# The sums of squares of queries and keys in the second block, as one full-precision matmul or as two rounded ones

## The chip, the cores and the metric

The kernel runs on one core of a Trainium2 chip. Its time is the device time of one execution in microseconds (us). Five engines work side by side, each in the order of its own program: TensorE (PE in the profile; its weight loads are PEld) multiplies, VectorE (DVE) and ScalarE (ACT) work on tiles, GpSimd (POOL) is a slower one of that kind, and SyncE (SP) issues the transfers from memory. They wait for each other by semaphores. Matmuls read the on-chip memory (SBUF) and write to the eight banks of PSUM; ACT and DVE take the results out of the banks.

## The reference

Two blocks stand behind each other: a mixer with a mixture of experts (32 experts, 256 tokens of 1024 numbers), and a second block with two kinds of attention and a feed-forward part. The change touches one step of the second block, the length to which the queries and keys of the gated delta rule are brought:

```python
def l2norm(x):
    xf = x.astype(jnp.float32)
    return xf * lax.rsqrt(jnp.sum(xf * xf, axis=-1, keepdims=True) + EPS_2)

proj = jnp.einsum('bsd,de->bse', hn, w_in[l])
(fq, fk, fv, ff, gq, gk, gv, ga, gb, gz, gate_fox, gate_gdn) = split_in(proj)
qkv = jax.nn.silu(causal_dwconv(jnp.concatenate([gq, gk, gv], axis=-1), gdn_conv_w[l]))
cq, ck, cv = jnp.split(qkv, [GDN_K_WIDTH, 2 * GDN_K_WIDTH], axis=-1)
q = l2norm(cq.reshape(B, S, GDN_HEADS, GDN_HEAD_K))
k = l2norm(ck.reshape(B, S, GDN_HEADS, GDN_HEAD_K))
```

There are 8 heads of 128 numbers and 256 tokens. The result goes on to the delta rule, then the outputs of both attentions to a projection and the feed-forward part.

## The kernel before, in words

The second block's attention part is the function `phase_c`. It goes through the 8 heads in two groups of 4 (`hg` is 0, then 1). In a group TensorE makes the projections in this order: gq, gk, gv (delta rule), fq, then the sums of squares ("ss"), then rows of gates spread over all partitions ("rb"), then fk, the products of keys and queries ("kq"), transposes, fv, gz, and behind them a chain of small matmuls that inverts a triangular matrix.

**Precise products from rounded parts.** Most large products are made in the rounded type (fp32r). A weight or an activation is taken apart into a high part (rounded) and a low part (what is left, rounded), and the product is three rounded matmuls. The weights come through SP's queue into a ring of two buffers and are taken apart unit by unit, each unit 128 x 1024: ACT makes the high part (L183, a cast), and the low part (L186, a subtraction) is made by VectorE for the even units and by GpSimd for the odd ones. High and low parts have four buffers each, so a cast waits until TensorE has used the unit four before it. `units.ahead(engine, who, n)` stands in each engine's program where that engine is to make the parts up to unit n + 3. A projection (`columns`) is four units. In the first group fq is units 12 to 15 and fk units 16 to 19, in the second group 40 to 43 and 44 to 47.

**The sums of squares.** The queries and keys, turned so that a head's 128 numbers lie in the partitions, are in `gT` (4 tiles of 128 x 512 for queries and keys of a group). ACT squares them (L1957) into `X` and `XT`, two tiles each, which `sq(j)` names. TensorE sums over the partitions with a matrix of ones (L2361). Both operands are plain fp32, and one such matmul is two MATMUL instructions in the trace. ACT turns the sums to 1/root by Ln (L1971) and Exp (L1975), and VectorE multiplies `gT` by it (L2206); TensorE needs that for kq, behind fk. TensorE's rb matmuls (L2367) come directly behind the sums and read only 8 rows of the array (8x512 operands).

**Order of the work around it.** All orders are written out by hand. ACT, behind the Silu of gv: 4 squares, cast of unit 17 (45), fq's first half out of its bank (L1964), casts of units 18 and 19 (46, 47), fq's second half, then Ln and Exp. VectorE: low part of units 16 and 18 (44 and 46), then the rows of rb (L2199), then L2206. GpSimd: low part of units 17 and 19 (45 and 47). `yf` and `yg` hold the outputs of the two attentions, each as a pair [0] (high) and [1] (low); the second half of their rows is first written at the end of the second group. `yf[0]` also serves early on for the parts of the small gate weights, which `wg2_high` and `wg2_low` name.

Of the kernel before, what the change touches and what calls it, by code (L numbers as in the profile page):

```python
# [27 lines left out]
F32 = mybir.dt.float32  # L28
F32R = mybir.dt.float32r
I32 = mybir.dt.int32  # L30
U32 = mybir.dt.uint32
ALU = mybir.AluOpType
# [3 lines left out]
P = 128  # L36
# [1606 lines left out]
HG = 4  # L1643
# [150 lines left out]
def phase_c(nc, A, sem, sb, ring, banks, k, env):  # L1794
    x, xn, hT, ident, tri, ones, sel, prm2, units, hTh, hTl, yf, yg, prm1, prow1, prow2, stat = (
        env[n] for n in "x xn hT ident tri ones sel prm2 units hTh hTl yf yg prm1 prow1 prow2 stat".split())
# [22 lines left out]
    def sq(j):  # L1819

        return (X, XT)[j // 2][:, j % 2].rearrange("p h n -> p (h n)")

    vb = sb("vb", [P, NT, HG, P])

    wg2 = X.rearrange("p t h n -> p (t h) n")
    wg2_high, wg2_low = (yf[0][:, 4 * i:4 * i + 4, :].rearrange("p c (a n) -> p (c a) n", a=2) for i in range(2))
# [41 lines left out]
    with nc.Block() as block:  # L1868
# [18 lines left out]
        def _(act):  # L1887
            chain = Chain(act, sem("actC"))
# [47 lines left out]
            for hg in range(2):  # L1936
# [19 lines left out]
                for j in range(4):  # L1956
                    act.activation(sq(j), gT[:, j // 2, 2 * (j % 2):2 * (j % 2) + 2, :].rearrange("p h s -> p (h s)"),  # L1957
                                   ACT.Square).then_inc(sem("g_sq"), 1)
                if hg == 0:
                    banks.moved(act, ("nm", KC // 2 - 1))  # L1960
                for j in range(2):
                    ahead(u0 + 12 + 2 * j + 2)
                    bank = banks.take(act, ("fq", hg, j))
# [5 lines left out]
                for j in range(4):  # L1969
                    bank = banks.take(act, ("ss", hg, j))  # L1970
# [7 lines left out]
                for h in range(HG):  # L1978
                    act.wait_ge(sem("dlog"), 4 * hg + h + 1)
                    act.activation(attnT[:, :, h, :], attnT[:, :, h, :], ACT.Exp).then_inc(sem("dexp"), 1)  # L1980
                    bank = banks.take(act, ("rb", hg, h))
                    act.activation(egb[:, h, :], bank[:, P:S], ACT.Exp).then_inc(sem("egb"), 1)
                for j in range(2):
                    ahead(u0 + 16 + 2 * j + 2)
                    bank = banks.take(act, ("fk", hg, j))
                    last = act.copy(fqk[:, 1, 2 * j:2 * j + 2, :], bank.rearrange("p (h s) -> p h s", h=2))
                    banks.release(last, ("fk", hg, j))
                for t in range(NT):
                    ahead(u0 + 20 + (3, 4)[t])
                    bank = banks.take(act, ("fv", hg, t))  # L1990
                    banks.release(act.copy(fv[:, t, :], bank), ("fv", hg, t))
                for t in range(NT):
                    bank = banks.take(act, ("x1", hg, t))
                    banks.release(act.copy(X[:, t], heads(bank)), ("x1", hg, t))
                for t in range(NT):
                    ahead(u0 + 24 + (3, 4)[t])
                    bank = banks.take(act, ("gz", hg, t))
                    banks.release(act.activation(gz[:, t, :], bank, ACT.Silu), ("gz", hg, t))
                for l in range(1, LEVELS):
                    for t in range(NT):  # L2000
                        bank = banks.take(act, ("t1", hg, l, t))
                        banks.release(act.copy(T1[:, t, :], bank), ("t1", hg, l, t))
                        if l > 1:
                            bank = banks.take(act, ("tr", hg, l, t))
                            banks.release(act.copy(XT[:, t], heads(bank)), ("tr", hg, l, t))

                for h in range(HG):
                    if h == HG - 1:
                        bank = banks.take(act, ("u0", hg))
                        banks.release(act.copy(u[:, 0], heads(bank)), ("u0", hg))  # L2010
                    act.wait_ge(sem("fmax"), 4 * hg + h + 1)
                    bank = banks.take(act, ("lo", hg, h))
# [5 lines left out]
                bank = banks.take(act, ("wT", hg))  # L2018
                banks.release(act.activation(wTn[:, :, :], heads(bank), ACT.Copy, scale=-1.0), ("wT", hg))
                bank = banks.take(act, ("st", hg))  # L2020
                banks.release(act.copy(state[:, :, :], heads(bank)), ("st", hg))
                bank = banks.take(act, ("u1", hg))
                banks.release(act.copy(u[:, 1], heads(bank)), ("u1", hg))
                for h in range(HG):
                    bank = banks.take(act, ("pt", hg, h))
                    banks.release(act.copy(probT[:, h, :], bank[:, 0:384]), ("pt", hg, h))
                for j in range(2):
                    bank = banks.take(act, ("pv", hg, j))
# [5 lines left out]
            for w, buf in (("gf", sgf), ("gg", sgg)):  # L2034
                for j in range(2):
                    ahead(UNITS_E + 4 * (w == "gg") + 2 * j + 2)
                    bank = banks.take(act, (w, 0, j))
# [8 lines left out]
        @block.gpsimd  # L2046
        def _(g):
            chain = Chain(g, sem("poolC"))
            g.wait_ge(sem("norm_scaled"), k.scaled("nm") + NT)
            units.ahead(g, "low1", -2)  # L2050
            g.memset(X[:, :, :, :], 0.0).then_inc(sem("wg2_zeroed"), 1)
            chain(g.memset(eps2[:, :], EPS2))
            chain(g.memset(lm[:, :, :], 0.0))
            for l in range(LEVELS):
                if l == 1:
                    g.wait_ge(sem("low0_split"), units.before["low0"] + 1)
                    units.ahead(g, "low1", 0)
                b = 1 << l
                odd = lm[:, l, :].rearrange("p (m o r) -> p m o r", o=2, r=b)[:, :, 1, :]
                m = P // (2 * b)  # L2060

                chain(g.memset(odd, -1.0))
                chain(g.affine_select(out=odd, in_=odd, compare_op=ALU.is_ge, fill=0.0, base=0,
                                      pattern=[[-2 * b, m], [0, b]], channel_multiplier=1))
                chain(g.affine_select(out=odd, in_=odd, compare_op=ALU.is_ge, fill=0.0, base=b - 1,
                                      pattern=[[2 * b, m], [0, b]], channel_multiplier=-1))
            mask_plain = vb[:, 0, 0, :]
            chain(g.memset(mask_plain, 0.0))
            chain(g.affine_select(out=mask_plain, in_=mask_plain, compare_op=ALU.is_ge, fill=-1e30, base=0,
                                  pattern=[[-1, P]], channel_multiplier=1))  # L2070
            chain.mark(g.tensor_copy(ident_r[:, :], ident[:, :]))
            g.tensor_copy(negmask[:, :], mask_plain).then_inc(sem("consts2"), 1)
            chain.wait()
            for hg in range(2):
                u0 = UNITS_GROUP * hg
                units.ahead(g, "low1", u0 + 20)
                g.wait_ge(sem("kk"), 4 * hg + 4)
                for l in range(LEVELS):
                    if l == 1:
                        units.ahead(g, "low1", u0 + 24)  # L2080
                    if l in (4, 5):
                        units.ahead(g, "low1", u0 + 24 + 2 * (l - 3))
                    if l in (2, 3):

                        for h in (2 * l - 4, 2 * l - 3):
                            banks.moved(g, ("kq", hg, h))
                            g.tensor_tensor(attnT[:, :, h, :], attnT[:, :, h, :],
                                            tri[:, :].unsqueeze(1).to_broadcast([P, NT, P]), ALU.mult)\
                                .then_inc(sem("attn_masked"), 1)
                    for t in range(NT):  # L2090
                        if l > 1:
                            banks.done(g, ("t1", hg, l - 1, t))
                        if l == 1:
                            g.wait_ge(sem("x1T"), NT * hg + t + 1)
                        g.tensor_tensor(heads(ATm[:, t, :]), AT[:, t], lm[:, l, :].unsqueeze(1).to_broadcast([P, HG, P]),
                                        ALU.mult).then_inc(sem("ATm"), 1)
            units.ahead(g, "low1", UNITS_E + 11)

        @block.vector
        def _(v):  # L2100
# [73 lines left out]
            for hg in range(2):  # L2174
# [14 lines left out]
                if hg == 0:  # L2189
# [2 lines left out]
                    banks.release(last, "cols")  # L2192
                    banks.moved(v, "cols")
                units.ahead(v, "low0", UNITS_GROUP * hg + 16)
                for h in range(HG):
                    bank = banks.take(v, ("rb", hg, h))
                    hh = HG * hg + h
                    for t in range(NT):
                        last = v.tensor_scalar(attnT[:, t, h, :], bank[:, t * P:(t + 1) * P], cols[:, t, hh:hh + 1], 0.0,  # L2199
                                               ALU.subtract, ALU.min)  # L2200
                    last.then_inc(sem("dlog"), 1)
# [95 lines left out]
        def _(pe):  # L2297
# [41 lines left out]
            for hg in range(2):  # L2339
# [16 lines left out]
                both_f(u0 + 12, "fq", hg)  # L2356

                for j in range(4):
                    pe.wait_ge(sem("g_sq"), 4 * hg + j + 1)
                    bank = banks.claim(pe, ("ss", hg, j))  # L2360
                    banks.filled(pe.matmul(bank, ones[:, 0:P], sq(j), start=True, stop=True), ("ss", hg, j))  # L2361

                pe.wait_ge(sem("row_low"), 2)
                for h in range(HG):
# [434 lines left out]
```

## Time and profile before

| | us |
|---|---|
| median of 3 runs | 1648.02 (1647.77 to 1649.14) |
| the profiled execution | 1648.02 |
| its span in the trace | 1646.3 |
| PE busy | 1624.4 (99%) |
| DVE busy | 613.7 (37%) |
| ACT busy | 475.8 (29%) |
| POOL busy | 302.4 (18%) |

The span goes from the first to the last instruction in the trace; 1.7 us of the execution lie outside it. "Busy" is the time in which an engine has an instruction under way; a matmul's recorded time goes on while the next one already runs, so rates are read from the starts. The granted clock (PEclk) is TensorE's: 1.00 is 2.4 GHz, 0.50 is 1.2 GHz. The second block's attention part lies from about 1043 us on, its first sums of squares at 1100 us and its second at 1239 us.

### The profile page before, as it was taken

The page shows a single profiled execution, that of the slowest core. Times are in us where ns is not written, and L with a number is a line of the kernel's source. Part 1 is how long each engine was busy: PE and PEld are TensorE (multiplying, and loading weights), DVE is VectorE, ACT ScalarE, POOL GpSimd, SP SyncE. Part 2 cuts the span into 40 slices and gives each one's busy share as a digit, 9 for nine tenths or more (in the row PEclk, how much of TensorE's full clock was granted, in tenths as well). Part 3 has the DMA queues.
Part 4 walks back from the last instruction along what each step waited for, and adds up shares of the span by engine and source line. Part 5 has one row for each costly group of instructions (what it writes and reads, how often), then busy time and mean ns, then how long its engine had stood idle before and what let it go on. Part 6 is the DMA issues. An engine that isn't in the chain of part 4 may idle for free. (4 is left out here: it accounts for less than half of the span.)

```text
span 1646.3 us, 22758 instructions
## 1 busy us (share of the span) xinstructions
PE 1624.4 (99%) x9272; PEld 946.4 (57%) x9272; DVE 613.7 (37%) x1144; ACT 475.8 (29%) x695; POOL 302.4 (18%) x192
## 2 busy tenths in 40 slices
PE   9999999999999999999999999999999999999998
PEld 8843333333333333333333333698998999999986
DVE  7743212112121212121121211675485244468852
ACT  5421110111111111111011111574555454454443
POOL 3500000000000000000000000535333624445552
PEclk9999999999999999999999999999999999999999
DMA  9698999999999999999999999353133215456552
GB/s 350 221 367 338 428 427 426 428 427 426 428 426 427 429 426 427 426 428 428 428 428 428 428 428 422 125 179 128 53 123 134 103 52 195 166 166 203 167 192 102
DMA packets 92919, 507.67 MB, mean 308 GB/s; under 512 B 8987, under 2 KB 32584, under 8 KB 68264
## 3 DMA queue, kind: packets, MB, share of 16 engines
q1 hardware_dynamic: 92696, 506.00, 76.1%
q8 instruction: 61, 1.00, 0.3%
q10 hardware_dynamic: 144, 0.52, 0.1%
q14 instruction: 18, 0.15, 0.0%
HBM read 505.46 MB, written 1.05 MB: 308 GB/s over the span
## 5 line engine op out<-in xcount | busy, mean ns | idle before, releaser
L186 POOL TENSOR_TENSOR low<-ring,high 128x1024 fp32r<-128x1024 f32 x81 | 199.6, 2465 | 1262.8 <-ACT high L183 1262.7
L1593 PE MATMUL ps<-ring,x 128*64 128x512 f32 x1536 | 337.5, 594 | 1.8 <-DMA ring<-in_w_up 1.8
L1593 PEld LDWEIGHTS ps<-ring,x 128*64 128x64 f32 x1536 | 108.0, 137 | 227.5 <-issue 222.4
L183 ACT CAST high<-ring 128x1024 fp32r<-128x1024 f32 x162 | 168.2, 1047 | 201.4 <-PE ps L1727 125.5
L1720 PE MATMUL ps<-hTh,high 128*128 128x256 f32 x800 | 198.8, 285 | 2.4 <-DVE hTl L633 1.9
L1721 PE MATMUL ps<-hTl,high 128*128 128x256 f32 x800 | 197.6, 284 | 0.0
L1626 PE MATMUL ps<-ring,x 128*64 128x512 f32 x752 | 171.7, 598 | 0.0
L186 DVE TENSOR_TENSOR low<-ring,high 128x1024 fp32r<-128x1024 f32 x81 | 111.1, 1371 | 146.7 <-ACT high L183 146.6
L1720 PEld LDWEIGHTS ps<-hTh,high 128*128 128x128 f32 x800 | 153.9, 192 | 4.2 <-issue 3.8
L1721 PEld LDWEIGHTS ps<-hTl,high 128*128 128x128 f32 x800 | 154.0, 192 | 0.0
L1466 DVE TENSOR_SCALAR hT<-ps 128x512 f32<-128x512 f32 x32 | 22.1, 692 | 295.8 <-PE ps L1593 295.8
L1593 PE MATMUL ps<-extra,x 128*64 128x512 f32 x512 | 113.8, 594 | 0.0
L1727 PE MATMUL ps<-hTh,low 128*128 128x256 f32 x784 | 110.8, 284 | 0.0
L1626 PEld LDWEIGHTS ps<-ring,x 128*64 128x64 f32 x752 | 49.8, 136 | 103.9 <-issue 103.9
L1727 PEld LDWEIGHTS ps<-hTh,low 128*128 128x128 f32 x784 | 101.9, 193 | 0.0
L1418 DVE TENSOR_TENSOR x<-ps,g 128x512 f32<-128x512 f32 x33 | 22.8, 692 | 204.3 <-PE ps L1559 204.3
L1531 ACT COPY hT<-ps 128x512 f32<-128x512 f32 x32 | 18.8, 586 | 261.5 <-PE ps L1626 261.5
L1526 ACT COPY gpickT<-ps 128x256 f32<-128x256 f32 x32 | 11.9, 372 | 251.5 <-PE ps L1606 251.5
L1522 ACT ACTIVATE hT<-hT 128x512 f32<-128x512 f32 x32 | 20.1, 630 | 220.9 <-DVE hT L1466 220.9
L1472 DVE TENSOR_SCALAR hT<-ps 128x512 f32<-128x512 f32 x32 | 22.1, 691 | 155.5 <-PE ps L1593 155.5
L1593 PEld LDWEIGHTS ps<-extra,x 128*64 128x64 f32 x512 | 36.0, 137 | 75.1 <-issue 74.4
L1568 PE MATMUL ps<-hT,gpickT 64*128 64x512 f32 x264 | 65.6, 615 | 0.7 <-ACT hT L1531 0.7
(465 smaller groups left out, 2181.7 us busy)
## 6 DMA issues: line engine op xcount, KB each, us to landing
ring<-in_w_down SPq DMA_DIRECT2D x52, 2048.0 KB, 20.5
ring<-in_w_gate SPq DMA_DIRECT2D x48, 2048.0 KB, 18.2
ring<-in_w_up SPq DMA_DIRECT2D x48, 2048.0 KB, 18.5
ring<-in_w_in SPq DMA_DIRECT2D x23, 2048.0 KB, 8.2
extra<-in_w_gate SPq DMA_DIRECT2D x16, 2048.0 KB, 18.9
extra<-in_w_up SPq DMA_DIRECT2D x16, 2048.0 KB, 17.5
extra<-in_w_down SPq DMA_DIRECT2D x14, 2048.0 KB, 21.0
ring<-in_w_up SPq DMA_DIRECT2D x22, 1024.0 KB, 7.4
```

The lines of the kernel that those rows point to most:

```text
L183: eng.copy(hi, self.raw(u)).then_inc(self.sem("high_split"), 1)
L186: eng.tensor_tensor(lo, self.raw(u), hi.bitcast(F32), ALU.subtract).then_inc(self.sem(who + "_split"), 1)
L1418: bank_free(v.tensor_tensor(xg[:, :, :, :], bank.rearrange("p (c h j) -> p c h j", c=4, h=2), gains, ALU.mult), G_)
L1466: bank_free(v.tensor_scalar(gt[:, :], bank, 7.0, None, ALU.min), GATE)
L1472: bank_free(v.tensor_scalar(up[:, :], bank, 7.0, -7.0, ALU.min, ALU.max), UP)
L1522: act.activation(sg[:, :], gt[:, :], ACT.Sigmoid, scale=1.702).then_inc(sem("sig"), 1)
L1568: last = pe.matmul(total(t, h), gpickT[h * CAP:(h + 1) * CAP, t, :], y[h * CAP:(h + 1) * CAP, :], start=False, stop=final)
L1593: last = pe.matmul(bank[h * CAP:(h + 1) * CAP, :], xg[:, c, kh, :], w[:, c, h * 512:(h + 1) * 512], start=False, stop=kh == 1 and c == 3)
L1626: last = pe.matmul(bank[h * CAP:(h + 1) * CAP, :], aT[:, c, kh, :], w[:, c, h * 512:(h + 1) * 512], start=False, stop=kh == 1 and c == 3)
L1720: pe.matmul(out, wh[:, w], xh[:, c, :], start=c == 0, stop=False)
L1721: last = pe.matmul(out, wh[:, w], xl[:, c, :], start=False, stop=False)
L1727: last = pe.matmul(out, wl[:, c * P:(c + 1) * P], xh[:, c, :], start=False, stop=c == KC - 1)
```

## The change

Each of the four tiles of squares of a group is taken apart into a rounded high part and a rounded low part, and TensorE sums these two with a rounded matrix of ones, `ones_r`, in two rounded matmuls instead of one fp32 matmul. ACT makes the high parts (four copies of 128 x 512 behind its squares), VectorE the low parts (four subtractions between its low parts of the weights and the rows of rb). The parts lie in the second halves of `yf` and `yg`. The squares' semaphore now counts 8 a group, and the low parts count on `wg2_low`.

```diff
+    def sq_part(i, j):
+
+        tile = (yf, yg)[j // 2][i][:, HG:, :].rearrange("p c s -> p (c s)")
+        return tile[:, (j % 2) * 512:(j % 2 + 1) * 512]
+
+    ones_r = sb("ones_r", [P, P], F32R)
...
                     act.activation(sq(j), gT[:, j // 2, 2 * (j % 2):2 * (j % 2) + 2, :].rearrange("p h s -> p (h s)"),
                                    ACT.Square).then_inc(sem("g_sq"), 1)
+                for j in range(4):
+                    act.wait_ge(sem("g_sq"), 8 * hg + j + 1)
+                    act.copy(sq_part(0, j), sq(j)).then_inc(sem("g_sq"), 1)
...
+            chain.mark(g.tensor_copy(ones_r[:, :], ones[:, 0:P]))
...
                 units.ahead(v, "low0", UNITS_GROUP * hg + 16)
+                for j in range(4):
+                    v.wait_ge(sem("g_sq"), 8 * hg + 4 + j + 1)
+                    v.tensor_tensor(sq_part(1, j), sq(j), sq_part(0, j).bitcast(F32), ALU.subtract)\
+                        .then_inc(sem("wg2_low"), 1)
...
                 for j in range(4):
-                    pe.wait_ge(sem("g_sq"), 4 * hg + j + 1)
+                    pe.wait_ge(sem("g_sq"), 8 * hg + 4 + j + 1)
                     bank = banks.claim(pe, ("ss", hg, j))
-                    banks.filled(pe.matmul(bank, ones[:, 0:P], sq(j), start=True, stop=True), ("ss", hg, j))
+                    pe.matmul(bank, ones_r[:, :], sq_part(0, j), start=True, stop=False)
+                    pe.wait_ge(sem("wg2_low"), 1 + 4 * hg + j + 1)
+                    banks.filled(pe.matmul(bank, ones_r[:, :], sq_part(1, j), start=False, stop=True), ("ss", hg, j))
```

TensorE, first group, before: the four sums of squares stand between the last unit of fq (L1727) and the rb matmuls (L2367).

```order
L1727 MATMUL ps<-hTh,low 128x256 x7
L2361 MATMUL ps<-X,ones 128x512 [waits bankC_free0,g_sq]
L2361 MATMUL ps<-X,ones 128x512 [waits bankC_free1,g_sq]
L2361 MATMUL ps<-XT,ones 128x512 [waits bankC_free2,g_sq]
L2361 MATMUL ps<-XT,ones 128x512 [waits bankC_free3,g_sq]
L2367 MATMUL ps<-row_high,sel 128x512 [waits bankC_free4,row_low]
```

The same place now, where `yf_high`/`yf_low` and `yg_high`/`yg_low` name the tiles with the parts of the squares:

```order
L1727 MATMUL ps<-hTh,low 128x256 x7
L2375 MATMUL ps<-yf_high,ones_r 128x512 [waits bankC_free0,g_sq]
L2377 MATMUL ps<-yf_low,ones_r 128x512 [waits wg2_low]
L2375 MATMUL ps<-yf_high,ones_r 128x512 [waits bankC_free1,g_sq]
L2377 MATMUL ps<-yf_low,ones_r 128x512 [waits wg2_low]
L2375 MATMUL ps<-yg_high,ones_r 128x512 [waits bankC_free2,g_sq]
L2377 MATMUL ps<-yg_low,ones_r 128x512 [waits wg2_low]
L2375 MATMUL ps<-yg_high,ones_r 128x512 [waits bankC_free3,g_sq]
L2377 MATMUL ps<-yg_low,ones_r 128x512 [waits wg2_low]
L2383 MATMUL ps<-row_high,sel 128x512 [waits bankC_free4,row_low]
```

Each low matmul has a wait of its own, for a subtraction on VectorE. ScalarE, first group, as it stands now, from the squares to the table load for Ln:

```order
L1963 ACTIVATE X<-gT 128x512 [waits g_silu]
L1963 ACTIVATE X<-gT 128x512
L1963 ACTIVATE XT<-gT 128x512 x2
L1967 CAST yf_high<-X 128x512 [waits g_sq] x2
L1967 CAST yg_high<-XT 128x512 [waits g_sq] x2
L183 CAST high<-ring 128x1024 [waits ringC_loaded0,bankC_full6,bankC_free3]
L1973 ACTIVATE hT<-ps 128x512 [waits bankC_full6]
L183 CAST high<-ring 128x1024 [waits ringC_loaded0,unit_used]
L183 CAST high<-ring 128x1024 [waits ringC_loaded0,bankC_full7]
L1973 ACTIVATE hT<-ps 128x512 [waits bankC_full7]
L1980 ACT_TABLE_LOAD [waits bankC_full0]
```

Only the four L1967 casts are new; what was behind the squares is now behind them. VectorE, first group, as it stands now, from the column copy to rb:

```order
L2201 COPY cols<-ps 128x48 [waits bankC_full5]
L186 TENSOR_TENSOR low<-ring,high 128x1024 [waits high_split,bankC_free5]
L186 TENSOR_TENSOR low<-ring,high 128x1024 [waits high_split]
L2207 TENSOR_TENSOR yf_low<-X,yf_high 128x512 [waits g_sq] x2
L2207 TENSOR_TENSOR yg_low<-XT,yg_high 128x512 [waits g_sq] x2
L2213 TENSOR_SCALAR xn<-ps,cols 128x128 [waits bankC_full4]
```

The four subtractions are new, and they stand behind the two low parts of weights (units 16 and 18), the second of which waits for ScalarE's cast of unit 18.

## Rows read from the trace of the kernel before

**Rows 1.** The page, part 1: busy time of each engine.
```profile
PE 1624.4 (99%) x9272; PEld 946.4 (57%) x9272; DVE 613.7 (37%) x1144; ACT 475.8 (29%) x695; POOL 302.4 (18%) x192
```

**Rows 2.** Waits of PE, 1040 to 1646 us: total, times, longest (one row of seven).
```profile
PE ps L1745 <- DVE xn L2227: 0.8, 1, 0.8
```

**Rows 3.** Timeline of PE, first group: start, length, instructions merged.
```profile
1100.50 1.88 PE L2361 MATMUL ps<-X,ones 128*128 128x512 f32 x4
1102.22 1.88 PE L2361 MATMUL ps<-XT,ones 128*128 128x512 f32 x4
1104.03 0.50 PE L2367 MATMUL ps<-row_high,sel 8*128 8x512 f32 x1
...
1104.61 0.39 PE L2367 MATMUL ps<-row_high,sel 8*128 8x512 f32 x1
1104.84 0.39 PE L2367 MATMUL ps<-row_low,sel 8*128 8x512 f32 x1
```

**Rows 4.** Timeline of PE, second group.
```profile
1238.62 1.88 PE L2361 MATMUL ps<-X,ones 128*128 128x512 f32 x4
...
1242.15 0.50 PE L2367 MATMUL ps<-row_high,sel 8*128 8x512 f32 x1
```

**Rows 5.** Timeline of ACT, first group.
```profile
1098.97 1.13 ACT L1957 ACTIVATE XT<-gT 128x512 f32<-128x512 f32 x2
1100.01 1.03 ACT L183 CAST high<-ring 128x1024 fp32r<-128x1024 f32 x1
...
1101.44 1.98 ACT L183 CAST high<-ring 128x1024 fp32r<-128x1024 f32 x2
1103.32 0.59 ACT L1964 ACTIVATE hT<-ps 128x512 f32<-128x512 f32 x1
```

**Rows 6.** Timeline of DVE, first group: in brackets, idle before and releaser.
```profile
1102.50 2.06 DVE L186 TENSOR_TENSOR low<-ring,high 128x1024 fp32r<-128x1024 f32 x1 [3.77 <-ACT high L183]
...
1109.62 2.50 DVE L2206 SCALAR_TENSOR_TENSOR gT<-gT,work 128x512 f32<-128x512 f32 x4 [2.66 <-ACT work L1975]
```

**Rows 7.** Timeline of POOL, first group.
```profile
1101.12 5.70 POOL L186 TENSOR_TENSOR low<-ring,high 128x1024 fp32r<-128x1024 f32 x2 [4.30 <-ACT high L183]
```

**Rows 8.** Line L186 on DVE: shortest, median, longest of an instruction, in ns.
```profile
L186 DVE TENSOR_TENSOR low<-ring,high x81: 1205/1225/3372, 1045.0 to 1627.5; 128x1024 fp32r<-128x1024 f32 x81
```

**Rows 9.** Timeline of DVE and POOL in the first block, 68 to 76 us.
```profile
68.94 4.93 DVE L266 TENSOR_TENSOR low_first<-ring,high_first 128x1024 fp32r<-128x1024 f32 x3 [4.50 <-ACT high_first L263]
...
71.19 1.60 POOL L892 TENSOR_TENSOR extra<-extra 128x256 f32<-128x256 f32 x1
...
75.41 0.74 POOL L892 TENSOR_TENSOR extra<-extra 128x256 f32<-128x256 f32 x1
```

**Rows 10.** Timeline of ACT, second group.
```profile
1233.76 1.03 ACT L183 CAST high<-ring 128x1024 fp32r<-128x1024 f32 x1
1234.69 0.58 ACT L1964 ACTIVATE hT<-ps 128x512 f32<-128x512 f32 x1
1235.95 1.05 ACT L183 CAST high<-ring 128x1024 fp32r<-128x1024 f32 x1 [0.67 <-PE ps L1727]
1238.83 1.04 ACT L183 CAST high<-ring 128x1024 fp32r<-128x1024 f32 x1 [1.83 <-PE ps L1727]
```

**Rows 11.** Timeline of DVE and POOL, second group.
```profile
1237.03 1.32 DVE L186 TENSOR_TENSOR low<-ring,high 128x1024 fp32r<-128x1024 f32 x1 [4.53 <-ACT high L183]
...
1234.87 2.40 POOL L186 TENSOR_TENSOR low<-ring,high 128x1024 fp32r<-128x1024 f32 x1 [4.00 <-ACT high L183]
1239.95 2.35 POOL L186 TENSOR_TENSOR low<-ring,high 128x1024 fp32r<-128x1024 f32 x1 [2.68 <-ACT high L183]
```

**Rows 12.** Stretches: length, busy PE PEld DVE ACT POOL, PEclk, DMA share, GB/s.
```profile
1240.00:1244.00 4.00, 4.00 (x14) 2.06 (x12) 1.08 (x5) 3.97 (x6) 2.29 (x1) 1.00 0.14 15
1244.00:1250.00 6.00, 6.00 (x38) 5.79 (x37) 3.58 (x9) 5.97 (x15) 0.00 (x0) 0.72 0.90 340
...
1640.00:1644.00 4.00, 0.00 (x0) 0.00 (x0) 2.32 (x5) 1.25 (x5) 0.00 (x0) 1.00 0.13 47
1644.00:1646.00 2.00, 0.00 (x0) 0.00 (x0) 0.00 (x0) 0.00 (x0) 0.00 (x0) 0.65 0.70 261
```

## The prediction

> **What bounds the kernel.** First the busy times on the page: PE is busy for 99% of the span, every other engine for 37% or less [rows 1]. Then the list of what PE waited for from 1040 us on: in the whole second block the row nearest behind the changed place is one wait of 0.8 us for VectorE's work on the kq banks [rows 2]. So TensorE sets the end, nearly without a gap. Two things follow. What TensorE no longer has to do is gained in full, and what it newly waits for is lost in full, because behind the changed place only 0.8 us of waiting is there to swallow a delay. Then the timelines of PE, ACT, DVE and POOL around 1100 us and 1239 us, the only two places that the change touches. What decides is not how busy VectorE is on average but where it stands when TensorE arrives.
>
> **What the matmuls themselves give.** A fp32 sum of squares is two instructions: four of them start at 1100.50 and the next four at 1102.22, so 0.43 us each and 0.86 a sum, 3.44 a group [rows 3]. A rounded 512-column matmul goes on to the next after 0.23 us (1104.61 to 1104.84; these have 8 rows of weights, but the same number of columns) [rows 3]. Eight of them are 1.84 us a group. The saving is 1.6 us a group, 3.2 us in all, if every operand is there. The Trainium skill ("TensorE: Matmul & The Clock Gate", back-to-back issue gap) gives columns by clock plus a small constant, 0.216 us for 512 columns; by it the saving would be 3.4 us instead of 3.2. The row is 7% longer, and I keep the row.
>
> **When the operands are there, first group.** Before, ACT had its four squares issued by 1100.01, and TensorE came to the sums at 1100.50 [rows 3, 5]. Now:
> - ACT: four copies of 128 x 512. The trace has no such copy from SBUF in the rounded type; two squares of that size take 1.04 us from 1098.97 to 1100.01, 0.52 each [rows 5]; half a 128 x 1024 cast would be 0.5. I take 0.52, 2.08 in all, and nothing hides it, since ACT works without a gap here. The cast of unit 17 moves from 1100.01 to 1102.09 and ends at 1103.12, that of unit 18 from 1101.44 to 1103.52 and ends about 1104.5, that of unit 19 ends about 1105.5.
> - POOL begins unit 17 0.08 us after that cast's end, as before (1101.12 against 1101.04 [rows 5, 7]): 1103.2, and needs 2.40 [rows 11]: until 1105.6.
> - DVE's unit 18 took 2.06 us instead of the usual 1.225 [rows 6, 8], and the two POOL units beside it took 5.70 instead of 2 x 2.4 [rows 7, 11]. The two engines took turns: POOL to 1103.5, DVE to 1104.56, POOL to 1106.82. So a subtraction with both inputs in SBUF on the one stops that on the other until it is over. Now unit 18 is free to go at 1104.5, waits for POOL until 1105.6, and ends 1.04 later, at 1106.6.
> - POOL's unit 19 has waited since 1105.6 and gets its turn before the first new subtraction: at 1106.6, for 2.26 us (1104.56 to 1106.82 before), to 1108.9. That a waiting POOL instruction slips in between two of VectorE's shows in the first block: three subtractions in a row on DVE take 4.93 us instead of about 3.5, while a POOL instruction that takes 0.74 alone takes 1.60 and ends at 72.79, in their midst [rows 9].
> - The four subtractions, each 128 x 512 with two inputs from SBUF: like L2206, 2.50 us for four [rows 6], so 0.60 to the next. They end at 1111.4, and with the last low matmul (0.23) the rb matmuls begin at 1111.7 instead of 1104.03 [rows 3]. That is a loss of 7.7 us, the saving already inside.
>
> The Trainium skill says of the pair of SBUF ports which VectorE and GpSimd share ("SBUF — State Buffer", the part on engine ports) that it goes whole to whichever instruction issues first and the other blocks to its end. The trace agrees (2.06 for 1.225 us). By it POOL's unit 19, which issues a microsecond before the first subtraction, goes first: that speaks for the 7.7 and against the 5.3 us of the rival below.
>
> **Second group.** Before, ACT had slack here: it waited for TensorE to free the units before two of its casts [rows 10]. The copies move the cast of unit 45 from 1233.76 to 1235.84, to end 1236.9; fq's half follows (0.4), unit 46 is cast from 1237.3 to 1238.3 instead of from 1235.95. Unit 47's cast stays where it is, at 1238.83, bound to TensorE [rows 10]. POOL has unit 45 from 1236.95 to 1239.35; DVE's unit 46 waits for that and ends at 1240.4; POOL's unit 47, ready at 1239.95, runs to 1242.7; the four subtractions end at 1245.2, and rb begins at 1245.5 instead of 1242.15 [rows 4]: a loss of 3.3 us.
>
> **The clock.** TensorE's clock was halved once in the second block, behind the sums and the rb matmuls of the second group: in the 6 us from 1244 the granted clock was 0.72, so 6 x 0.28 = 1.7 us were lost [rows 12]. It came after 1.9 us of 8-row matmuls without any idle time. And at the end TensorE stands still from 1640; the clock is full to 1644 and falls before 1646 [rows 12]. In the changed kernel TensorE stands still in the first group from 1100.7 to about 1109.5, 8.8 us, longer than it took at the end; so the clock falls, and rb, at 1.84 us or twice that, stands directly behind. Bounds: nothing, if it is back before rb; twice the 1.7 us of the one fall shown, if rb keeps it down. I take 2.5, between one such stretch and two, as both causes come together. In the second group TensorE stands still for 4.5 us, and the fall shown is there already; bounds are -1.7 (it doesn't come again) and +1.7 (it lasts twice as long); I take +0.8.
>
> **What else moves.** The 0.8 us wait [rows 2] goes: the DVE work before it is late by about 6 us, TensorE by more. Ln, Exp and L2206 in the first group shift by less than TensorE itself, and L2206 ended at 1112.1 while kq comes behind fk, 11.5 us after rb: covered. The copy of `ones_r` on POOL is once and early: 0. SP's queue waits for the low parts of older pieces and PE waited for no transfer in this block: 0.
>
> **Sum.** 7.7 + 3.3 + 2.5 + 0.8 - 0.8 = 13.5 us, on the profiled execution's own 1648.02 (span 1646.3 and 1.7 around it), which is also the median: 1661.5 us.
>
> **Rivals.**
> - *VectorE goes first.* If the subtractions follow on unit 18 without letting POOL in, they end at 1109.1 and 1242.9, rb begins at 1109.4 (+5.3) and 1243.2 (+1.0). With 2.5 for the clock and -0.8: +8.0, 1656.0 us. For it: they are issued back to back. Against: the case of [rows 9].
> - *The saving comes out.* If all eight low parts are ready when TensorE arrives, the kernel gains 3.2 us: 1644.8, and 1.7 less if the clock stays up. It decides by whether the last subtraction ends by about 1102 and 1240. Against: the four subtractions alone are 2.4 us, behind a cast that was not over before about 1102.4 even in the kernel before (the first of the two from 1101.44 [rows 5]), and the four copies come on top.
> - *The delay is swallowed.* If the shift of TensorE meets waits which the waits list does not show as such, or the clock does not fall, the total is near 0 to +3: 1648 to 1651. Against: 0.8 us of waits [rows 2].
> - *It goes on.* The shift of POOL and DVE, or a longer half clock, makes further waits at kq and in the triangular chain, some 4 to 6 us more: 1667.
>
> **Chances.** Forecast 0.58, its own range 1658 to 1664 (10.2 us without the clock, and clock terms from -1.7 to +5.1 in all, of which I leave out what lies below 0). VectorE first 0.22; it goes on 0.12; the saving comes out 0.04; the delay is swallowed 0.04. The range of 1655 to 1666.5 holds the first two and part of the third. This kernel's runs can be told apart by 0.2%, 3.3 us: faster than that 0.04, within it 0.05 (part of the saving, part of the swallowed), slower 0.91.
>
> **What would show it.** On PE, an idle time of 8 to 9 us before the first L2377 with VectorE's L2207 as the releaser, and one of 4 to 5 us in the second group; between the later low matmuls starts 0.6 us apart. On DVE, unit 18 at about 1104.5 lasting 2.1 us, and the first L2207 lasting about 2.9 instead of 0.7 us, because it waits for POOL (with *VectorE first* it lasts 0.7). On ACT, the four L1967 at 0.52 us. A granted clock of 0.5 over the rb matmuls of the first group. The forecast is wrong if PE's idle time before L2377 is under 5 us in the first group, if the stretch from there to fk runs at clock 1.00, or if PE's waits later in the block shrink by more than 1 us.

## Result, and the profile after

The changed kernel takes 1663.24 us (median of 4 runs, 1660.16 to 1664.86) against 1647.95 before (4 runs): ratio 1.0090, 95% interval 1.0078 to 1.0102. It is slower by 15.3 us; 1661.5 was forecast, with a range of 1655 to 1666.5. The profiled execution took 1664.21 us (span 1662.5).

First the list of what PE waited for from 1040 us on, the two longest of seven. The wait of [rows 2] is no longer in it; the other waits of before are.

```profile
PE ps L2377 <- DVE yf_low L2207: 12.5, 2, 8.3
PE ps L1720 <- DVE hTl L633: 1.9, 2, 1.0
```

Then PE's timeline in the first group, which answers to [rows 3]; fq's last low matmuls begin at 1100.88 where they began at 1099.55 before.

```profile
1100.88 1.12 PE L1727 MATMUL ps<-hTh,low 128*128 128x256 f32 x8
1102.01 0.49 PE L2375 MATMUL ps<-yf_high,ones_r 128*128 128x512 f32 x1
1110.77 0.79 PE L2377 MATMUL ps<-yf_low,ones_r 128*128 128x512 f32 x1 [8.27 <-DVE yf_low L2207]
1111.36 0.63 PE L2375 MATMUL ps<-yf_high,ones_r 128*128 128x512 f32 x1
1111.79 0.63 PE L2377 MATMUL ps<-yf_low,ones_r 128*128 128x512 f32 x1
...
1114.05 0.79 PE L2383 MATMUL ps<-row_high,sel 8*128 8x512 f32 x1
```

One high matmul, then 8.3 us of nothing, then rounded matmuls that start 0.43 us apart, nearly twice the 0.23 of [rows 3]; the granted clock there is 0.50 (the stretches further down). Who was late is read on the other engines. ACT, the same stretch (for [rows 5]):

```profile
1100.31 1.13 ACT L1963 ACTIVATE XT<-gT 128x512 f32<-128x512 f32 x2
1101.35 1.12 ACT L1967 CAST yf_high<-X 128x512 fp32r<-128x512 f32 x2
1102.38 1.13 ACT L1967 CAST yg_high<-XT 128x512 fp32r<-128x512 f32 x2
1103.42 1.04 ACT L183 CAST high<-ring 128x1024 fp32r<-128x1024 f32 x1
```

The four casts take 1101.35 to 1103.42, 2.07 us, and what was behind the squares is late by that. DVE and POOL (for [rows 6, 7]):

```profile
1105.92 2.05 DVE L186 TENSOR_TENSOR low<-ring,high 128x1024 fp32r<-128x1024 f32 x1 [5.84 <-ACT high L183]
1107.89 3.42 DVE L2207 TENSOR_TENSOR yf_low<-X,yf_high 128x512 fp32r<-128x512 f32 x2
1111.24 1.28 DVE L2207 TENSOR_TENSOR yg_low<-XT,yg_high 128x512 fp32r<-128x512 f32 x2
```

```profile
1104.54 5.63 POOL L186 TENSOR_TENSOR low<-ring,high 128x1024 fp32r<-128x1024 f32 x2 [6.38 <-ACT high L183]
```

Two subtractions of the same size take 3.42 us and then 1.28. By line (shortest, median, longest in ns) it is the first one of each group:

```profile
L2207 DVE TENSOR_TENSOR yf_low<-X,yf_high x4: 678/1750/2821, 1107.9 to 1252.4; 128x512 fp32r<-128x512 f32 x4
L2207 DVE TENSOR_TENSOR yg_low<-XT,yg_high x4: 679/679/679, 1111.2 to 1253.6; 128x512 fp32r<-128x512 f32 x4
```

It lies blocked behind POOL's unit 19 (47 in the second group) for 2.1 of its 2.8 us. The second group, DVE, POOL and PE (for [rows 4, 11]):

```profile
1247.67 2.10 DVE L186 TENSOR_TENSOR low<-ring,high 128x1024 fp32r<-128x1024 f32 x1 [5.83 <-ACT high L183]
1249.69 3.42 DVE L2207 TENSOR_TENSOR yf_low<-X,yf_high 128x512 fp32r<-128x512 f32 x2
1253.04 1.28 DVE L2207 TENSOR_TENSOR yg_low<-XT,yg_high 128x512 fp32r<-128x512 f32 x2
```

```profile
1249.30 2.67 POOL L186 TENSOR_TENSOR low<-ring,high 128x1024 fp32r<-128x1024 f32 x1 [0.61 <-ACT high L183]
```

```profile
1252.57 0.79 PE L2377 MATMUL ps<-yf_low,ones_r 128*128 128x512 f32 x1 [4.21 <-DVE yf_low L2207]
...
1255.85 0.79 PE L2383 MATMUL ps<-row_high,sel 8*128 8x512 f32 x1
```

And the stretches with the granted clock (third number from the end), for [rows 12]:

```profile
1104.00:1110.00 6.00, 0.00 (x0) 0.00 (x0) 4.08 (x2) 3.32 (x5) 5.44 (x2) 0.55 0.24 87
1110.00:1114.00 4.00, 3.23 (x7) 2.14 (x7) 2.52 (x4) 2.35 (x3) 0.17 (x1) 0.50 0.65 208
1114.00:1120.00 6.00, 6.00 (x38) 5.23 (x38) 4.66 (x12) 5.97 (x13) 0.00 (x0) 0.93 0.57 213
1250.00:1252.00 2.00, 0.00 (x0) 0.00 (x0) 2.00 (x1) 0.00 (x0) 1.97 (x1) 0.84 0.00 0
1252.00:1264.00 12.00, 11.43 (x36) 9.03 (x37) 7.16 (x16) 9.06 (x18) 0.00 (x0) 0.50 0.51 175
1264.00:1266.00 2.00, 2.00 (x15) 2.00 (x15) 0.00 (x0) 0.92 (x1) 0.00 (x0) 0.75 0.00 0
```

In the first group the clock is back 0.9 us into the rb matmuls; in the second it stays at 1.2 GHz through the sums, rb and the first 5 us of fk.

**Where the 16.2 us of the profiled execution lie**, by the starts of the same matmuls in both traces. The first kq matmul of each group, before:

```profile
1117.71 3.74 PE L2378 MATMUL ps<-gT 128*128 128x128 f32 x32
1257.31 3.74 PE L2378 MATMUL ps<-gT 128*128 128x128 f32 x32
```

After:

```profile
1128.07 3.73 PE L2394 MATMUL ps<-gT 128*128 128x128 f32 x32
1273.55 3.74 PE L2394 MATMUL ps<-gT 128*128 128x128 f32 x32
```

| from | to | before, us | after, us | difference |
|---|---|---|---|---|
| start of span | fq's last low matmuls | 1099.55 | 1100.88 | +1.3 |
| there | first rb matmul | 4.48 | 13.17 | +8.7 |
| there | first kq matmul | 13.68 | 14.02 | +0.3 |
| there | second group's sums | 120.91 | 119.90 | -1.0 |
| there | first rb matmul | 3.53 | 7.88 | +4.3 |
| there | first kq matmul | 15.16 | 17.70 | +2.5 |
| there | last matmul | 382.25 | 382.20 | 0 |

The first 1.3 us have nothing to do with the change: in this execution the clock fell once in the first block, where no instruction has changed. The stretch 42 to 48 us, first in the kernel before, then after:

```profile
42.00:48.00 6.00, 6.00 (x26) 4.91 (x27) 5.36 (x13) 2.36 (x4) 2.40 (x1) 1.00 1.10 411
```

```profile
42.00:48.00 6.00, 6.00 (x21) 4.76 (x20) 4.08 (x9) 1.85 (x3) 2.39 (x1) 0.72 1.09 404
```

Of the 6 x 0.28 = 1.7 us of clock that these cost, 1.3 reach the second block. The same fall (0.72 from 42 to 48 us) stands in the profiled executions of four of the nine kernels below and not in those of the other five, although no instruction of that part differs in any of them; it is a part of the spread between runs.

### The profile page after: what moved, and what is told of

Read it like the earlier page. It is cut to its first block and busy times, and to the rows that moved or that the text cites. A ratio compares the mean times of both kernels' runs of the same rounds, so it can differ in the third digit from the quotient of the medians.

```text
span 1662.5 us, 22775 instructions
## 1 busy us (share of the span) xinstructions
PE 1628.8 (98%) x9272; PEld 951.2 (57%) x9272; DVE 622.9 (37%) x1152; ACT 480.1 (29%) x703; POOL 302.6 (18%) x193
## 5 line engine op out<-in xcount | busy, mean ns | idle before, releaser
L186 POOL TENSOR_TENSOR low<-ring,high 128x1024 fp32r<-128x1024 f32 x81 | 199.6, 2465 | 1280.3 <-ACT high L183 1280.2
L186 DVE TENSOR_TENSOR low<-ring,high 128x1024 fp32r<-128x1024 f32 x81 | 109.7, 1355 | 153.7 <-ACT high L183 153.6
L1727 PE MATMUL ps<-hTh,low 128*128 128x256 f32 x784 | 110.8, 284 | 0.0
L1727 PEld LDWEIGHTS ps<-hTh,low 128*128 128x128 f32 x784 | 101.9, 193 | 0.0
```

The costliest lines, as they stand in the source:

```text
L186: eng.tensor_tensor(lo, self.raw(u), hi.bitcast(F32), ALU.subtract).then_inc(self.sem(who + "_split"), 1)
L1727: last = pe.matmul(out, wl[:, c * P:(c + 1) * P], xh[:, c, :], start=False, stop=c == KC - 1)
```

## Experiments

All are edits of the changed kernel unless said otherwise. Times are medians, ratios are to runs of the kernel before that were made beside them (medians 1648.03, 1648.28 and 1648.37 us). Where traces are compared, it is one profiled execution of each kernel.

**The subtractions ahead of unit 18.** VectorE's program in each group:

```diff
-                units.ahead(v, "low0", UNITS_GROUP * hg + 16)
+                units.ahead(v, "low0", UNITS_GROUP * hg + 13)
                 for j in range(4):
                     v.wait_ge(sem("g_sq"), 8 * hg + 4 + j + 1)
...
+                units.ahead(v, "low0", UNITS_GROUP * hg + 16)
```

> VectorE's four subtractions stand ahead of its low part of unit 18 (46) instead of behind it; everything else is as in the changed kernel. My theory: TensorE's wait comes from what the subtractions queue behind. Then they follow the copies, end near 1103.2 in the first group and 1236.9 in the second (times of the kernel before), rb begins 0.5 us earlier than before the change and 1.6 us earlier in the second group, and the clock falls no more than before; ACT's chain to the kq banks is still 2 us late, which lengthens the one 0.8 us wait there to as much as 3. Together 1646 to 1650 us. Rival, that rounded matmuls or the copies themselves cost the time: it stays at 1658 or more. Rival, that the half clock alone is the loss: TensorE's idle time at the low matmuls stays near 8 us.

1649.39 us, ratio 1.0010 (1.0001 to 1.0019). The place of four instructions of VectorE is worth 14 us. PE's long waits are gone, and two short ones are new, which stand in its timeline:

```profile
1106.42 0.50 PE L2384 MATMUL ps<-row_high,sel 8*128 8x512 f32 x1 [0.74 <-ACT hT L1973]
...
1108.42 0.38 PE L1720 MATMUL ps<-hTh,high 128*128 128x256 f32 x1 [1.27 <-ACT work L1980]
```

I had looked for ACT's delay at the kq banks; it comes earlier. The fourth rb matmul pair needs the bank of fq's second half, which ACT empties 2 us late, and fk needs the bank that ACT's Ln frees. The clock fell behind these waits (3.4 us at half), and for another 3.4 us in the second group, as in the kernel before.

**GpSimd gives way.** Its low part of unit 19 (47) waits for the subtractions:

```diff
+                units.ahead(g, "low1", u0 + 14)
+                g.wait_ge(sem("wg2_low"), 1 + 4 * hg + 4)
                 units.ahead(g, "low1", u0 + 20)
```

> GpSimd waits for the four subtractions before its low part of unit 19 (47), so it can't slip in ahead of them. My theory (the two engines take turns at subtractions with two inputs in SBUF): the first L2207 lasts 0.7 instead of 2.8 us, TensorE's waits for it shrink by about 2.1 us in each group, 8.3 to 6.2 and 4.2 to 2.1, and the clock comes back a little earlier: 4 to 7 us off the changed kernel, 1656 to 1659 us. Rival, that the first subtraction was long for another reason (its own start, the write to another tile): no change, 1663.

1660.16 us, ratio 1.0077 (1.0061 to 1.0092). The waits are as the turns foretell: PE's waits for L2209 (the same subtractions), and their lengths on DVE.

```profile
PE ps L2379 <- DVE yf_low L2209: 8.2, 2, 6.1
```

```profile
L2209 DVE TENSOR_TENSOR yf_low<-X,yf_high x4: 677/678/679, 1107.2 to 1251.0; 128x512 fp32r<-128x512 f32 x4
```

12.5 us of waits became 8.2, and no subtraction is longer than 0.68. The whole gained only 3.1 us, less than the 4 to 7 expected, and with four runs of each kernel that overlap (up to 1661.22 here, from 1660.16 there) the times alone do not settle it; the waits and the lengths do. In the first group the half clock now lasted for 13.7 us (1106.4 to 1120.1) instead of 10.2, and took back part of the gain; in the second it lasted 3.4 instead of 13.7.

**Filler matmuls during the waits.**

```diff
                     bank = banks.claim(pe, ("ss", hg, j))
+                    if j == 0:
+                        keep_busy(pe, bank, ones, 8 if hg else 17)
                     pe.matmul(bank, ones_r[:, :], sq_part(0, j), start=True, stop=False)
```

> The changed kernel with matmuls of ones during TensorE's two waits: 17 fp32 matmuls of 256 columns (0.43 us each, 7.3 us) ahead of the first group's sums and 8 (3.4 us) ahead of the second's; their results are overwritten. The waits stay, only the clock is held. My theory: the half clock costs 1.6 us in the first group and 3.8 in the second over the waits themselves, so 1663.2 becomes 1656 to 1658, with a granted clock of 1.00 over rb and fk in both groups. Rival, that the clock costs next to nothing because TensorE waits anyway: 1663.

1658.37 us, ratio 1.0068 (1.0053 to 1.0084): 4.9 us less by doing more (four runs each, the slowest here 1660.09, the fastest of the changed kernel 1660.16). From fq's last low matmuls to the last matmul its trace is 6.4 us shorter. Its clock stayed up through both groups:

```profile
1100.00:1114.00 14.00, 13.04 (x58) 9.74 (x57) 8.05 (x11) 9.91 (x16) 5.65 (x2) 1.00 0.58 210
1240.00:1262.00 22.00, 21.23 (x143) 18.60 (x142) 12.65 (x19) 17.97 (x32) 5.42 (x3) 1.00 0.50 181
```

Its trace gives the waits free of the clock, by the first rb matmul of each group:

```profile
1111.81 0.49 PE L2385 MATMUL ps<-row_high,sel 8*128 8x512 f32 x1
1252.25 0.49 PE L2385 MATMUL ps<-row_high,sel 8*128 8x512 f32 x1
```

In the first group rb starts 7.8 us later than the 1104.03 of before, and the work ahead of it lay 0.1 later: 7.7 us. From there to the second group's rb it takes 2.3 us more than before, with the wait at kq's bank gone (1.0): 3.3 us.

**Only ACT's part early.** Squares ahead of the first Silu of gv, copies ahead of the second; the subtractions stay behind unit 18:

```diff
                 for w in range(3):
...
+                        if w == 2:
+                            (squares, square_parts)[j](hg)
                         banks.moved(act, (("gq", "gk", "gv")[w], hg, j))
```

> Only ACT's squares and copies are moved to their early places; VectorE's subtractions stay behind the low part of unit 18 (46). It tells ACT's part of the delay from VectorE's place. My theory: ACT's casts are back at their times of before; in the first group the subtractions still stand behind unit 18 and GpSimd's unit 19 (until 1106.8), end at 1109.3 and rb is 5.5 us late with 1 to 2 for the clock; in the second, VectorE has ended unit 46 at 1238.35, before GpSimd's unit 47, so that the subtractions end at 1240.8 and rb is 1.0 us earlier than before the change: 1651 to 1655 us. Rival, that ACT's 2.1 us are all of it: 1645 to 1648. Rival, that they are no part of it: 1663.

1657.66 us, ratio 1.0061 (1.0044 to 1.0078), above the range expected. ACT's delay is a part of the loss, VectorE's place the larger one: PE still waits 4.4 and 2.0 us. In the second group I had the subtractions end before POOL's unit 47. They did not:

```profile
1246.11 1.28 DVE L2215 TENSOR_TENSOR yf_low<-X,yf_high 128x512 fp32r<-128x512 f32 x2
1247.31 3.44 DVE L2215 TENSOR_TENSOR yg_low<-XT,yg_high 128x512 fp32r<-128x512 f32 x2
```

```profile
1247.78 2.43 POOL L186 TENSOR_TENSOR low<-ring,high 128x1024 fp32r<-128x1024 f32 x1 [2.67 <-ACT high L183]
```

POOL's unit 47 came up at 1247.78, while the third was under way, and the fourth took 2.8 us. In the changed kernel the turn came ahead of the first of the four, here ahead of the last. The rest of the miss is the clock: the first group ran at half for 10.2 us and lost 3.3 from rb to kq.

**All of the added work, fp32 matmuls, no wait for the parts.**

```diff
-                    pe.wait_ge(sem("g_sq"), 8 * hg + 4 + j + 1)
+                    pe.wait_ge(sem("g_sq"), 8 * hg + j + 1)
                     bank = banks.claim(pe, ("ss", hg, j))
-                    pe.matmul(bank, ones_r[:, :], sq_part(0, j), start=True, stop=False)
-                    pe.wait_ge(sem("wg2_low"), 1 + 4 * hg + j + 1)
-                    banks.filled(pe.matmul(bank, ones_r[:, :], sq_part(1, j), start=False, stop=True), ("ss", hg, j))
+                    banks.filled(pe.matmul(bank, ones[:, 0:P], sq(j), start=True, stop=True), ("ss", hg, j))
```

> All of the added work on ACT, VectorE and GpSimd as in the changed kernel, but TensorE makes the sums as before, with one fp32 matmul from the fp32 squares, and waits for none of the parts, which are made for nothing. My theory: without the wait the two idle times of 8.3 and 4.2 us are gone and the clock falls no more than before; VectorE is still late with rb's rows (its subtractions end 7 us later than it began on them before), which lengthens the one 0.8 us wait at the kq banks by up to 4 us in the first group: 1648 to 1653 us. Rival, that the added work on the two engines is itself the cost: about 1663.

1650.66 us, ratio 1.0015 (1.0005 to 1.0025). So the added work alone costs 2.4 us, not 15. The place that I expected was wrong again: TensorE did not wait at kq but for ACT, 0.4 us at rb and 1.2 us at fk, with 6.8 us of half clock.

**Without the low pass** (no subtractions, no low matmuls; the sums are of the high parts alone):

```diff
-                    pe.matmul(bank, ones_r[:, :], sq_part(0, j), start=True, stop=False)
-                    pe.wait_ge(sem("wg2_low"), 1 + 4 * hg + j + 1)
-                    banks.filled(pe.matmul(bank, ones_r[:, :], sq_part(1, j), start=False, stop=True), ("ss", hg, j))
+                    banks.filled(pe.matmul(bank, ones_r[:, :], sq_part(0, j), start=True, stop=True), ("ss", hg, j))
```

> The low pass is left out (no subtractions, no low matmuls, no wait for them), so the sums are those of the rounded high parts alone. ACT's copies stay where the change puts them. My theory: TensorE waits for copies only, under 1 us; rb begins 1.6 us earlier than before the change in the first group and 2.6 in the second; ACT is still 2.1 us late at Ln and Exp, which costs up to 3 us at the kq banks: 1644 to 1648 us. Rival, that the copies in front of ACT's casts are the main loss: over 1655.

1649.94 us, ratio 1.0011 (1.0001 to 1.0020): a miss upward by 2 us. The sums were 1.5 and 2.5 us shorter than before, and TensorE then waited at rb and fk for ACT, 3.3 us in both groups, with 6.8 us of half clock in the first group. The saving on TensorE brought nothing here while ACT, 2 us late, held the next banks. The first group:

```profile
1107.38 0.50 PE L2377 MATMUL ps<-row_high,sel 8*128 8x512 f32 x1 [1.64 <-ACT hT L1973]
...
1109.38 0.58 PE L1720 MATMUL ps<-hTh,high 128*128 128x256 f32 x1 [1.07 <-ACT work L1980]
```

**Both early.** ACT as in the kernel with its part early, and VectorE's subtractions directly behind gv's convolution:

```diff
                 conv(2, "gv", hg)
+                for j in range(4):
+                    v.wait_ge(sem("g_sq"), 8 * hg + 4 + j + 1)
+                    v.tensor_tensor(sq_part(1, j), sq(j), sq_part(0, j).bitcast(F32), ALU.subtract)\
+                        .then_inc(sem("wg2_low"), 1)
```

> ACT squares ahead of the first Silu of gv and makes the rounded copies ahead of the second, where it has idle times of 3.0 and 2.1 us; VectorE subtracts directly behind the convolution of gv, ahead of both low parts of weights. The same instructions as in the changed kernel, in other places. My theory: all eight parts are ready when TensorE comes, so the saving of the matmuls is what is left: 3.2 us below the kernel before, 1644.8 us, and up to 1.7 less if the clock no longer falls. Rival, that the added work on ACT or VectorE costs time wherever it stands: between 1648 and 1663. Rival, that two rounded matmuls are not cheaper than one in fp32: 1648.

1645.85 us, ratio 0.9989 (0.9980 to 0.9998), 11 runs against 21: 2.2 us faster than before the change and 17 faster than the changed kernel, with the same instructions. PE's timeline in the first group, as the change meant it:

```profile
1100.73 0.40 PE L2383 MATMUL ps<-yf_high,ones_r 128*128 128x512 f32 x1
1100.96 0.40 PE L2385 MATMUL ps<-yf_low,ones_r 128*128 128x512 f32 x1
...
1102.66 0.50 PE L2391 MATMUL ps<-row_high,sel 8*128 8x512 f32 x1
```

Eight matmuls 0.23 us apart, rb 1.93 us behind the first instead of 3.53. TensorE got the 3.2 us, but ran into a wait of 0.7 us in each group (before: one of 0.8):

```profile
PE ps L1745 <- DVE xn L2249: 1.4, 2, 0.7
```

**Both early, fp32 matmuls.** The same, with the PE edit of *all of the added work* above.

```diff
-                    pe.matmul(bank, ones_r[:, :], sq_part(0, j), start=True, stop=False)
...
+                    banks.filled(pe.matmul(bank, ones[:, 0:P], sq(j), start=True, stop=True), ("ss", hg, j))
```

> The same early places of squares, copies and subtractions, but TensorE makes the sums with one fp32 matmul each from the fp32 squares, as before the change; the parts are made for nothing. It measures the matmuls alone against the early kernel. My theory: the saving of 1.6 us a group is real and TensorE's only gain, less the 0.7 us wait that the faster sums ran into: 1.8 to 3.2 us above the early kernel, 1647.7 to 1649 us, the same as the kernel before, with VectorE's and ACT's added work hidden in full. Rival: the early places themselves, not the matmuls, gave the gain: 1646.

1646.35 us, ratio 0.9989 (0.9980 to 0.9998). That misses the 1647.7 to 1649 expected and is the rival's 1646: by medians this version is 0.5 us above the rounded one, which the intervals do not separate, so the medians do not show that the matmuls gave the gain. The traces do show the saving:

```profile
1101.35 1.88 PE L2383 MATMUL ps<-X,ones 128*128 128x512 f32 x4
...
1104.87 0.50 PE L2389 MATMUL ps<-row_high,sel 8*128 8x512 f32 x1
```

The sums take 3.52 instead of 1.93 us a group, 3.2 in all. Against it stand the rounded version's waits at L1745, 1.4 us, which this version does not have. From fq's last low matmuls to the last matmul the rounded one takes 1.3 us less (536.2 against 537.5).

What hides this in the medians is the clock. Each run has a mean granted clock. At 0.999 this version takes 1645.6 to 1646.5 us (7 runs) and the rounded one 1644.0 and 1644.4; at 0.998 it is 1647.1 and 1647.5 against 1645.3 and 1645.8, at 0.997 it is 1647.9 and 1648.3 against 1645.5 and 1645.9. At equal clock the rounded one is 1.8 to 2.4 us faster, of which 0.3 may come from the two sets of runs; the clock is known to a thousandth only, which is itself 1.6 us, so this is an indication. But this version ran at 0.999 in 7 of 11 runs, the rounded one in 2 of 11 and the kernel before, beside them, in 2 of 21. This fits with this version coming out below the kernel before: in its profiled execution the wait of 0.8 us and the fall of the clock in the second group are gone. Why the clock stays up more often with it is not shown.

**Both early, and unit 22 behind the kq work.** VectorE's low part of unit 22 (50) took 3.4 us instead of 1.2, blocked by POOL, in front of the kq banks (the longest of [rows 8]):

```diff
-                units.ahead(v, "low0", UNITS_GROUP * hg + 20)
                 for h in range(HG):
                     banks.moved(v, ("rb", hg, h))
...
                     banks.release(last, ("kq", hg, h))
+                units.ahead(v, "low0", UNITS_GROUP * hg + 20)
```

> As the kernel with squares, copies and subtractions early, and VectorE's low part of unit 22 (50), which lay blocked by GpSimd for 3.4 us ahead of the kq work, now stands behind that work. My theory (turns at the shared inputs again, and TensorE's two waits of 0.7 us at fv's first bank come from them): both waits go, 1.4 us below the early kernel, about 1644.5 us; it would be the fastest of all. Rival: the low part of unit 22 is then late for fv itself and TensorE waits there instead: 1645.9 or more.

1645.34 us, ratio 0.9980 (0.9971 to 0.9989): the fastest median, 3.0 us below before, 0.5 us below the early kernel, which the intervals do not separate (in the traces it is 1.9 us from fq's last low matmuls to the last matmul). PE's list of waits from 1066 us on has no L1745 any more; its longest row is

```profile
PE ps L1720 <- DVE hTl L633: 1.0, 1, 1.0
```

## Why the prediction held, step by step

| term | forecast | measured | where |
|---|---|---|---|
| rb late, first group, clock aside | +7.7 | +7.5 (filler kernel: +7.7) | last subtraction |
| rb late, second group, clock aside | +3.3 | +3.1 (filler kernel: +3.3) | last subtraction |
| clock, first group | +2.5 | about +1.5 | table: 8.7 + 0.3 - 7.5 |
| clock, second group | +0.8 | about +3.7 | table: 4.3 + 2.5 - 3.1 |
| the wait at kq's bank goes | -0.8 | -1.0 | table |
| sum | 13.5 | 14.9 (unrounded), and 1.3 of the first block | table |

For the first two rows I take the end of the last subtraction in the changed kernel's own trace, 1112.52 and 1254.32, less the shift that TensorE had come with (1.33 and 9.35), and 0.3 to rb: 1111.5 and 1245.3, 7.5 and 3.1 us later than before. The clock terms are what the table of starts has beyond them. The two errors in them partly offset each other (1.0 too much in the first group, 2.9 too little in the second), so the sum is closer than its terms.

*The steps on ACT, VectorE and GpSimd* were right to 0.3 us: four copies 2.07 us (2.08 said), unit 18 2.05 us long (2.1), the first subtraction 2.82 (2.9). *VectorE first* is out: GpSimd took its turn in both groups. That these turns are the cause of 2.1 us a group is shown by making GpSimd wait (12.5 to 8.2 us of waits in the trace); that the place behind unit 18 is the cause of most of it, by moving the subtractions in front (1649.39).

*The saving comes out* was the right mechanism in the wrong order of instructions: with everything early it is there in the trace, 1.6 us a group, as worked out. How much of the 2.2 us gained over the kernel before comes from it is open: with the same early places and fp32 matmuls the median gain is 2.0.

*The mis-sized term is the clock in the second group.* I wrote that it would cost 0.8 us over the fall already there, with 1.7 as the upper bound. It cost 3.7: the array ran at 1.2 GHz for 12.4 us of work. The bound came from one fall of 3.4 us behind busy work, and one such fall was no measure for a fall behind an idle time: here, behind 4.2 us of it, the granted clock stayed at 0.50 through the sums, the 8-row matmuls and the start of fk. What held it down is not shown. In the first group I had the same thought and the clock was back sooner than I took it, 0.9 us into rb. The shorter wait thus had the longer half clock, and with GpSimd giving way it was the other way round (13.7 us at half behind 6.1 us in the first group, 3.4 behind 2.1 in the second), so a clock term behind such a wait is uncertain by several us. The changed kernel's runs spread over 4.7 us, the 4 of before over 1.4, and the spread goes with the clock: the mean granted clock is 0.995 in the run of 1660.16, 0.993 in that of 1662.27, and 0.991 and 0.992 in the two slowest. The filler kernel shows that holding the clock is worth 4.9 us by medians.

*What I left out:* ACT's delay of 2.07 us reaches TensorE at rb's fourth pair and at fk's first bank. In the changed kernel the longer wait hides it. As soon as that was taken away it cost 2.0 us of waits (the kernel with the subtractions first) and 3.3 (no low pass), and with the half clock that came with them they ate the saving. So *What TensorE no longer has to do is gained in full* did not hold either: the list of waits shows no wait that is hidden behind TensorE's own work.

## What to carry to other kernels

Four cheap instructions on an engine that is 37% busy cost 14 us, because they stood behind a wait in their queue: a new operand for the bound engine is placed by when its inputs are there (in the early kernel the squares begin 10.9 us before the sums) and by where the other engines have idle time, not beside the work it is used with. Check each bank that a delayed engine still holds, in the order in which the bound engine claims them, not only the one with a wait in the list. And price an idle time on TensorE at more than its length: here 12.5 us of waits came with 5.2 us lost to the half clock (1.5 and 3.7 in the table).

## What the hardware showed that I had not expected

- A turn at the shared inputs was given to GpSimd inside a back-to-back run of VectorE's two-input subtractions, not only at its start: the fourth of four took 2.8 instead of 0.68 us when GpSimd's came up. The Trainium skill ("SBUF — State Buffer", "Who interferes with whom") has the one that issues first go first and the other block for the whole instruction; the traces agree, and they add that a run of short instructions did not keep the inputs.
- The half clock, from the fall of the granted clock to its return, lasted 3.4, 6.8, 10.2 or 13.7 us in different versions and groups. Its length did not follow the idle time: 8.3 us of idle time was followed by 10.2 and 4.2 by 13.7 (changed kernel), 6.1 by 13.7 and 2.1 by 3.4 (GpSimd gives way), 4.4 by 10.2 (only ACT's part early).
- Matmuls whose results nobody uses, put into the two waits, made the kernel 4.9 us faster (1663.24 to 1658.37).
